# A four-layer transformer kernel: first tiles walked by halves, GpSimd's additions spread, squares moved, small squares by blocks, another table of steps

## What is computed

```python
def first_block(x, ...):                                  # layers 0 and 1
    for l in range(DEPTH):
        proj = x @ w_in[l]
        hq, hf, hi, hg, nq, kc, vc, ks, vs, kw, vw, gt = jnp.split(proj, pts, axis=-1)
        o_a = hgrn2_mixer(hq, hf, hi, hg, lbs[l], hg_norm_w[l])   # gated linear recurrence, 4 heads of 128
        o_b = nsa_mixer(nq, kc, vc, ks, vs, kw, vw, gt, ...)      # compressed, selected and window attention
        mix = jnp.concatenate([o_a, o_b], axis=-1) @ w_out[l]
        x = layer_norm(ALPHA * x + mix, ln1_g[l], ln1_b[l])
        ffn = (jax.nn.silu(x @ w_ffn_gate[l]) * (x @ w_ffn_up[l])) @ w_ffn_down[l]
        x = layer_norm(ALPHA * x + ffn, ln2_g[l], ln2_b[l])

def second_block(x, ...):                                 # layers 2 and 3
    for layer in range(DEPTH):
        h = rmsnorm(x, attn_norm[layer])
        ...                                               # q, k, v (and the index network in layer 2)
        x = x + mixed @ w_o[layer]
        h = rmsnorm(x, ffn_norm[layer])
        x = x + conv_ffn(h, w_up[layer], conv_w[layer], conv_b[layer], w_down[layer])   # width 2816
    return rmsnorm(x, final_norm)
```

## Time and profile before

| what | before |
|---|---|
| median of 3 runs | 1427.36 us (1426.35 to 1429.48) |
| profiled execution, its own time | 1427.59 us |
| its span | 1425.8 us |
| mean granted clock of TensorE | 0.989 |
| busy share: TensorE, VectorE, ScalarE, GpSimd | 96%, 67%, 51%, 6% |
| DMA | 233 MB, 164 GB/s |

### The profile page before, as it was taken

How to read it: one execution, slowest core, us unless ns; L and a number is a source line. 1 busy time by engine, 2 the same in 40 slices (tenths; PEclk the granted TensorE clock), 3 DMA queues, 4 the chain that set the end, 5 groups by cost and what they waited for, 6 DMA issues and landing times.

```text
span 1425.8 us, 24726 instructions
## 1 busy us (share of the span) xinstructions
PE 1368.6 (96%) x10094; PEld 1257.3 (88%) x10094; DVE 956.0 (67%) x1624; ACT 729.5 (51%) x1216; POOL 84.1 (6%) x79
## 2 busy tenths in 40 slices
PE   9998899999999988999998999999999999999998
PEld 7997689999899868999988988889999998889997
DVE  5676775555759576655565786687777655687776
ACT  4755444333475644343354555655546555655554
POOL 0330000000004100000000011220000000000000
PEclk9999999999999999999998999999999999999999
DMA  8752245555443314655534434445554534545541
GB/s 315 280 179 78 87 155 194 185 178 181 155 196 120 118 60 148 212 195 183 178 122 159 149 119 148 140 174 178 182 192 167 202 105 145 191 154 201 180 177 59
DMA packets 38632, 233.24 MB, mean 164 GB/s; under 512 B 5016, under 2 KB 8808, under 8 KB 12152
## 3 DMA queue, kind: packets, MB, share of 16 engines
q1 hardware_dynamic: 36456, 224.18, 45.2%
q0 software_dynamic: 2064, 7.47, 1.6%
HBM read 230.55 MB, written 1.09 MB: 162 GB/s over the span
## 4 chain that ended last, share of the span: by engine, by line
PE 81%; DVE 11%; ACT 4%; issue 2%; DMA 1%; POOL 0%; SPq 0%; DVEq 0%; ACTq 0%
PE bank L776 20%; PE bank L777 19%; PE bank L778 19%; PE bank L784 4%; PE bank L785 4%; PE bank L788 4%; DVE w_lo L603 3%; PE bank L899 2%; PE bank L984 1%; ACT w_hi L593 1%; PE bank L1006 1%; PE bank L1019 1%; DVE arena L1755 1%; DVE heads_buf L1588 1%; DVE x L1704 1%
## 5 line engine op out<-in xcount | busy, mean ns | idle before, releaser
L603 DVE TENSOR_TENSOR w_lo<-raw,w_hi 128x1024 fp32r<-128x1024 f32 x404 | 483.7, 1236 | 99.7 <-ACT w_hi L593 95.3
L776 PE MATMUL bank<-a_hi,w_hi 128*128 128x256 f32 x1856 | 529.8, 285 | 6.6 <-DVE w_lo L603 6.1
L777 PE MATMUL bank<-a_lo,w_hi 128*128 128x256 f32 x1856 | 525.8, 283 | 0.0
L778 PE MATMUL bank<-a_hi,w_lo 128*128 128x256 f32 x1856 | 525.6, 283 | 0.0
L593 ACT ACTIVATE w_hi<-raw 128x1024 fp32r<-128x1024 f32 x404 | 406.3, 1050 | 94.5 <-PE bank L778 67.4
L776 PEld LDWEIGHTS bank<-a_hi,w_hi 128*128 128x128 f32 x1856 | 356.6, 192 | 12.3 <-issue 8.9
L777 PEld LDWEIGHTS bank<-a_lo,w_hi 128*128 128x128 f32 x1856 | 356.8, 192 | 1.3
L778 PEld LDWEIGHTS bank<-a_hi,w_lo 128*128 128x128 f32 x1856 | 356.7, 192 | 0.0
L1755 DVE SCALAR_TENSOR_TENSOR arena<-bank,conv_col,arena 128x254 f32<-128x254 f32 (+1 forms) x176 | 76.7, 477 | 51.8 <-ACT arena L1313 50.1
L784 PE MATMUL bank<-w_hi,a_hi 128*128 128x256 f32 (+1 forms) x320 | 100.6, 335 | 5.9 <-ACT a_hi L619 2.3
L777 PE MATMUL bank<-w_lo,h_hi 128*128 128x512 f32 x264 | 105.2, 399 | 0.0
(11 more groups left out here) (266 smaller groups left out, 1892.1 us busy)
## 6 DMA issues: line engine op xcount, KB each, us to landing
raw<-in_stream SPq DMA_DIRECT2D x201, 1024.0 KB, 4.9
bias_t<-bias_rows SPq DMA_DIRECT2D x6, 512.0 KB, 6.9
heads_buf<-in_w SPq DMA_DIRECT2D x2, 1024.0 KB, 8.0
gains<-in_w SPq DMA_DIRECT2D x2, 1024.0 KB, 10.0
gains<-in_ln_g POOLq DMA_DIRECT2D x4, 512.0 KB, 4.2
gains<-in_ln_b POOLq DMA_DIRECT2D x4, 512.0 KB, 5.9
gains<-in_rms_g POOLq DMA_DIRECT2D x3, 512.0 KB, 4.3
res<-in_xT SPq DMA_DIRECT2D x4, 256.0 KB, 5.0
```

Source lines behind the costliest of these rows:

```text
L603: dve.tensor_tensor(w_lo[:, i % PARTS, half_tile(h)], raw[:, i % SLOTS, half_tile(h)], w_hi[:, i % PARTS, half_tile(h)].bitcast(F32), ALU. ...
L776: pe.matmul(out, lh, rh, start=first, stop=False)
L777: pe.matmul(out, lh, rl, start=False, stop=False)
L778: return pe.matmul(out, ll, rh, start=False, stop=last)
```

## The change

The table of steps changes in all four layers; the order of the weight stream does not. `WARM` goes from 7 to 4. `first_rows` becomes `first_tiles`: tile hi0 for both row halves together, by halves of the weight tile, all products with the high weight part before those with the low one; tile hi1 in the same way for the first and then the second row half. The last warm-up matmul leaves its sum open, and tile hi0 adds to the zeros. At levels 2 and 3 (halves of 64 and 32) only the kept blocks are multiplied: 8 matmuls of 64 x 64 and 16 of 32 x 32 instead of 8 of 128 x 128. At the norm between layers 1 and 2 ScalarE squares after one weight tile's split instead of after two. GpSimd's addition h waits for hidden tile 3 + h of layer 2's feed-forward part.

```diff
--- before.py
+++ after.py
@@ -37,7 +37,7 @@
 SLOTS = 3
 X_PARTS = 4
 HID_PARTS = 4
-WARM = 7
+WARM = 4
 PARTS = 3
 HSLOTS = 6
 HEAD = 2
@@ -91,33 +91,33 @@
     0: """
         a hf0, b hf0, a hf1, b hf1, a hq0, gates, b hq0, logs, a hq1, sums, b hq1, a kskw, decay 1, b kskw,
         a nq0, decay 2, level 0, b nq0, level 1, a kcvc, level 2, b kcvc, level 3, a hg0, level 4, b hg0,
-        level 5, gt, a hg1, level 6, b hg1, hid 0, level 7, hid 1, level 8, silu, a vsvw, hid 2, phase
-        heads, hid 3, ho 0, ho 1, b vsvw, hidT, a nq1, gtT, S 0, kcv, S 1, ho_out, b nq1, oT 0, T 0, phase
+        gt, level 5, a hg1, level 6, b hg1, hid 0, level 7, hid 1, level 8, silu, a vsvw, hid 2, phase
+        heads, ho 0, hid 3, b vsvw, ho 1, hidT, a nq1, S 0, kcv, S 1, gtT, ho_out, b nq1, oT 0, T 0, phase
         out, oT 1, out 0 0 0, S 2, T 1, out 0 0 1, V 0, V 1, S 3, out 1 0 0, T 2, S 4, phase out1, out 1 0
-        1, cs, V 2, T 3, out 0 1 0, V 3, S 5, out 0 1 1, T 4, cT, S 6, out 1 1 0, V 4, co 0, co 1, out 1 1
-        1, T 5, S 7, mT 2, V 5, T 6, out 2 0 0, out 2 0 1, T 7, out 2 1 0, V 6, V 7, mT 3, out 2 1 1""",
+        1, cs, V 2, T 3, out 0 1 0, V 3, S 5, out 0 1 1, cT, T 4, S 6, out 1 1 0, V 4, co 0, co 1, T 5, S 7,
+        mT 2, out 1 1 1, V 5, T 6, out 2 0 0, out 2 0 1, T 7, out 2 1 0, V 6, V 7, out 2 1 1, mT 3""",
     1: """
-        a hf0, b hf0, a hf1, b hf1, a hq0, gates, logs, b hq0, a hq1, b hq1, sums, a kskw, b kskw, a nq0, b
-        nq0, decay 1, level 0, decay 2, a kcvc, level 1, b kcvc, level 2, a hg0, level 3, b hg0, gt, level
-        4, a hg1, level 5, level 6, hid 0, b hg1, level 7, a vsvw, silu, level 8, hid 1, hid 2, phase heads,
-        ho 0, b vsvw, ho 1, hid 3, gtT, S 0, hidT, S 1, a nq1, ho_out, kcv, b nq1, T 0, phase out, oT 0, S
-        2, out 0 0 0, oT 1, V 0, T 1, out 0 0 1, out 1 0 0, V 1, S 3, T 2, S 4, out 1 0 1, phase out1, cs, V
-        2, out 0 1 0, S 5, T 3, out 0 1 1, T 4, V 3, S 6, cT, V 4, out 1 1 0, out 1 1 1, co 0, T 5, mT 2, co
-        1, V 5, S 7, T 6, out 2 0 0, T 7, V 6, out 2 0 1, V 7, out 2 1 0, mT 3, out 2 1 1""",
+        a hf0, b hf0, a hf1, b hf1, a hq0, gates, logs, b hq0, a hq1, b hq1, a kskw, sums, b kskw, a nq0,
+        decay 1, b nq0, level 0, decay 2, a kcvc, level 1, b kcvc, level 2, a hg0, level 3, b hg0, gt, hid
+        0, level 4, a hg1, level 5, level 6, b hg1, level 7, a vsvw, silu, level 8, hid 1, hid 2, phase
+        heads, ho 0, gtT, b vsvw, ho 1, hid 3, S 0, hidT, S 1, a nq1, ho_out, kcv, b nq1, T 0, phase out, oT
+        0, S 2, out 0 0 0, oT 1, V 0, T 1, out 0 0 1, out 1 0 0, V 1, S 3, T 2, S 4, out 1 0 1, phase out1,
+        cs, V 2, out 0 1 0, S 5, T 3, out 0 1 1, T 4, V 3, S 6, cT, V 4, out 1 1 0, out 1 1 1, co 0, T 5, mT
+        2, co 1, V 5, S 7, T 6, out 2 0 0, T 7, V 6, out 2 0 1, V 7, out 2 1 0, mT 3, out 2 1 1""",
     2: """
         phase tiles, kw, a qi0, b qi0, kwT, a qi1, b qi1, a qi2, kiT, b qi2, I 0, I 1, a qi3, b qi3, I 2, I
-        3, a q0, b q0, I 4, I 5, a k0, I 6, b k0, I 7, S 0, a q1, choose 0 2, b q1, T 0, choose 0 2, a k1, S
-        1, V 0, choose 0 2, b k1, T 1, S 2, a q2, choose 0 2, V 1, choose 1 2, T 2, b q2, V 2, choose 1 2, S
-        3, a k2, b k2, choose 1 2, choose 1 2, unsel, a v2, T 3, S 4, V 3, b v2, T 4, a q3, S 5, V 4, b q3,
-        T 5, a k3, V 5, mT 0, b k3, a v3, S 6, mT 1, b v3, out 0 0 0, phase out, S 7, out 0 0 1, T 6, out 1
-        0 0, out 1 0 1, V 6, mT 2, T 7, phase out1, out 0 1 0, out 0 1 1, V 7, out 1 1 0, out 1 1 1, mT 3,
+        3, a q0, I 4, b q0, I 5, a k0, I 6, I 7, b k0, S 0, a q1, choose 0 2, b q1, choose 0 2, T 0, a k1, S
+        1, choose 0 2, choose 0 2, b k1, V 0, S 2, T 1, a q2, V 1, T 2, b q2, choose 1 2, V 2, choose 1 2, S
+        3, a k2, b k2, choose 1 2, T 3, a v2, choose 1 2, unsel, V 3, S 4, b v2, T 4, a q3, S 5, V 4, b q3,
+        T 5, a k3, V 5, mT 0, b k3, a v3, S 6, b v3, mT 1, phase out, S 7, out 0 0 0, T 6, out 0 0 1, out 1
+        0 0, out 1 0 1, mT 2, V 6, T 7, phase out1, out 0 1 0, out 0 1 1, V 7, out 1 1 0, out 1 1 1, mT 3,
         out 2 0 0, out 2 0 1""",
     3: """
-        phase tiles, a q0, b q0, a k0, b k0, S 0, a q1, b q1, T 0, a k1, S 1, b k1, V 0, T 1, S 2, V 1, a
-        q2, b q2, S 3, T 2, a k2, b k2, T 3, S 4, a v2, V 2, V 3, b v2, T 4, a q3, V 4, S 5, b q3, T 5, a
-        k3, mT 0, b k3, V 5, S 6, a v3, b v3, mT 1, phase out, S 7, T 6, out 0 0 0, out 0 0 1, out 1 0 0,
-        out 1 0 1, V 6, mT 2, out 0 1 0, T 7, phase out1, out 0 1 1, V 7, out 1 1 0, out 1 1 1, mT 3, out 2
-        0 0, out 2 0 1""",
+        phase tiles, a q0, b q0, a k0, b k0, a q1, S 0, b q1, T 0, a k1, S 1, V 0, b k1, T 1, S 2, V 1, a
+        q2, b q2, S 3, T 2, a k2, b k2, T 3, S 4, a v2, V 2, V 3, b v2, T 4, a q3, V 4, S 5, b q3, a k3, T
+        5, mT 0, b k3, V 5, S 6, a v3, b v3, mT 1, phase out, S 7, T 6, out 0 0 0, out 0 0 1, out 1 0 0, out
+        1 0 1, out 0 1 0, V 6, mT 2, T 7, phase out1, out 0 1 1, V 7, out 1 1 0, out 1 1 1, mT 3, out 2 0 0,
+        out 2 0 1""",
 }
 
 
@@ -815,21 +815,31 @@
                     mm = high_first(out, tiles[4 * q:4 * q + 4], lambda: wait_drained(pe, turned), q == 0, q == 1)
                 return mm
 
-            def first_rows():
-
-
-                b = open_bank((0, "hi0"))
+            def first_tiles():
+
+
+
+                banks = [open_bank((0, name)) for name in HEAD_TILES[0]]
                 pe.wait_ge(zeroed, 1)
-                for _ in range(WARM):
-                    pe.matmul(b[:, 0:512], s_hg[:, 0:P], s_hg[:, 0:512], start=True, stop=True)
-                w = [part[:, 0, :].rearrange("p (k c) -> p k c", k=KT) for part in (w_hi, w_lo)]
-                for k in range(KT):
-                    if k % 2 == 0:
-                        pe.wait_ge(a_lo_done, k // 2 + 1)
-                    if k % 4 == 0:
-                        pe.wait_ge(w_lo_done, k // 4 + 1)
-                    products(b[:, 0:S], (a_hi[:, k, 0:P], a_lo[:, k, 0:P]), [part[:, k, :] for part in w],
-                             k == 0, k == KT - 1)
+                for n in range(WARM):
+                    pe.matmul(banks[0][:, 0:512], s_hg[:, 0:P], s_hg[:, 0:512], start=True, stop=n < WARM - 1)
+                for i, rows in ((0, (0, 1)), (1, (0,)), (1, (1,))):
+                    high, low = [part[:, i, :].rearrange("p (k c) -> p k c", k=KT) for part in (w_hi, w_lo)]
+                    for h in range(2):
+                        pe.wait_ge(w_hi_done, 2 * i + h + 1)
+                        places = [(k, slice(tt * P, (tt + 1) * P), banks[i][:, tt * S:(tt + 1) * S])
+                                  for k in range(4 * h, 4 * h + 4) for tt in rows]
+                        for n, (k, t, out) in enumerate(places):
+                            if i == 0 and n % 4 == 0:
+                                pe.wait_ge(a_lo_done, k // 2 + 1)
+                            pe.matmul(out, a_hi[:, k, t], high[:, k, :], start=i > 0 and k == 0, stop=False)
+                            pe.matmul(out, a_lo[:, k, t], high[:, k, :], start=False, stop=False)
+                        pe.wait_ge(w_lo_done, 2 * i + h + 1)
+                        for k, t, out in places:
+                            mm = pe.matmul(out, a_hi[:, k, t], low[:, k, :], start=False,
+                                           stop=(k, t.start) == (KT - 1, rows[-1] * P))
+                    if rows[-1] == NT - 1:
+                        close_bank(mm)
 
             def behind_norm_tiles(n, keys, heads):
 
@@ -896,7 +906,13 @@
                         continue
                     for st in range(NT):
                         c = h * S + st * P
-                        mm = pe.matmul(out[:, c:c + P], lhs[:, c:c + P], rhs[:, c:c + P], start=True, stop=True)
+                        if half not in BY_BLOCKS:
+                            mm = pe.matmul(out[:, c:c + P], lhs[:, c:c + P], rhs[:, c:c + P], start=True, stop=True)
+                            continue
+                        for at in range(0, P, 2 * half):
+                            keys, queries = slice(c + at, c + at + half), slice(c + at + half, c + at + 2 * half)
+                            mm = pe.matmul(out[at:at + half, queries], lhs[:, keys], rhs[:, queries],
+                                           start=True, stop=True)
                 mm.then_inc(product_done, 1)
 
             def compress(l, part):
@@ -1141,11 +1157,7 @@
                 if l > 0:
                     pe.wait_ge(acc_drained, 2 * l * PIECES)
 
-            first_rows()
-            half_of_tile((0, "hi0"), True)
-            for name in HEAD_TILES[0][1:]:
-                half_of_tile((0, name), False)
-                half_of_tile((0, name), True)
+            first_tiles()
 
             pe.wait_ge(start_in, STARTS)
             b = open_bank(("cmpbias",))
@@ -1275,10 +1287,13 @@
                 keys, turn = norm_tail(l, kind), norms[-1]
                 act.activation(nstat[:, 0, 18:19], eps_ln[:, 0:1], ACT.Sqrt)
```

(8 more changed lines are left out.)

## The result

| what | before | after |
|---|---|---|
| median | 1426.86 us (4 runs, 1423.35 to 1429.48) | 1414.59 us (4 runs, 1413.50 to 1416.32) |
| profiled execution; its span | 1427.59; 1425.8 us | 1413.50; 1411.7 us |
| mean granted clock | 0.989 | 0.991 |

The ratio is 0.9915, with a 95% interval of 0.9897 to 0.9933: faster by 12.3 us, where 11.1 were predicted. The two profiled executions lie 14.1 us apart: that of the changed kernel is its fastest run, and that of the kernel before lies 0.7 us above its median.

A forecast was written before the change was run, and what follows sets the result against it. TensorE, with a matmul in flight 96% of the span, was taken as the bound. Terms -2.8 - 1.9 - 2.2 - 1.1 - 3.1 = -11.1 from 1427.59 gave 1416.4 us for the median; range 1412.5 to 1420, widened to 1410.5 to 1421.5.

The forecast's parts named there:

- start: First tiles: fewer warm-ups and a new product order bring line 1156 from 22.36 to about 19.5 us; -2.8 us.
- squares: Levels with halves of 64 and 32: multiplying only kept blocks saves 1.9 us over two layers, mostly at 64.
- norm: Between layers 1 and 2: squaring after one split starts the transposes 2.1 us earlier, head tiles 2.3; term -2.2 us.
- additions: Layer 2's feed-forward part: spreading GpSimd's additions stops them slowing VectorE ahead of h_hi; -1.1 us.
- table: Attention parts of all four layers: reordered steps cover TensorE's waits, -1.0, -0.5, -1.2, -0.4 by layer; -3.1 us.
- the idle pieces of 0.7 and 0.3 us: First tile: TensorE idles 0.7 us for the next a_lo part and 0.3 us for the second high half.
- at 0.055 ... the 32-level 1.76 (saves 0.03): Squares: at 0.055 us a record, from two nearest rows, the 32-level costs 1.76 us and saves only 0.03.
- The low end, -3.6: Squares, two layers: if cost went with columns (0.028 us a record), the 32-level would save 0.89 too; -3.6 us.
- The bound of -4: Norm between layers 1 and 2: less idle time may also avoid the first of two clock drops, each up to 1.7 us.
- the other fourteen or so are hidden by VectorE's idle quarter: Layer 2's feed-forward part: from up6 on splits are 3 us and more ahead, so the remaining spread additions cost nothing.
- the wait at T 4: Layer 2 attention: the softmax of S 4, which had 1.5 us of cover before T 4, has none.
- T 0 now has 2.9 us where it needs about 3.5: Layer 3 attention: T 0 has too little time behind S 0, set against 0.7 us gained at S 0; net -0.4.

The follow-up runs named there:

- experiment 7: Changed kernel with experiment 6's edit, plus only 32 x 32 diagonal blocks multiplied in ten of the twelve masked levels: 1408.60 us, ratio 0.9870.
- Experiment 5: Changed kernel with both high weight splits ahead of the squares again at the norm between layers 1 and 2: 1417.85 us, ratio 0.9935.
- experiment 4: Changed kernel with GpSimd's sixteen additions in one block again: 1416.00 us, ratio 0.9920.
- experiment 8: Kernel before the change with only the new table of steps: 1423.62 us beside 1429.19, ratio 0.9970.
- experiment 6: Changed kernel with layer 0's mT 3 back ahead of the last output piece (out 2 1 1): 1414.30 us, ratio 0.9914.
- experiment 3: Changed kernel with the former table of steps in all layers: 1420.65 us, ratio 0.9957.
- experiment 1: Changed kernel with the start undone (seven warm-up matmuls, first tile row half after row half): 1418.06 us, ratio 0.9938.
- experiment 2: Changed kernel with whole 128 x 128 squares at levels 2 and 3 again: 1418.77 us, ratio 0.9938.
- experiment 9: Changed kernel with 45 unused identity matmuls filling TensorE's idle time ahead of transposes at four norms: 1412.37 us, ratio 0.9890.

## Why the prediction was nearly right, and where not

The forecast of 1416.4 lies 1.8 us above the median and inside its range; the mechanism (each part takes a wait or columns away, and nearly all of it arrives) held. One term was clearly mis-sized: the squares saved 3.4 us by the rows, not 1.9, which is nearly the whole miss. The other rows stand within 0.3 us of their terms, two of them by errors that cancel.

| term | predicted | undone, by medians (by ratios) | gain in the pair of traces |
|---|---|---|---|
| start | -2.8 | 3.5 (3.3) | 2.8 at the small product |
| squares | -1.9 | 4.2 (3.3) | 1.7 a layer |
| norm | -2.2 | 3.3 (2.9) | 2.2 at the first set, 2.5 at the second |
| additions | -1.1 | 1.4 (0.7) | 0.8 over the part (undone 0.15) |
| table | -3.1 | 6.1 (6.0), alone 4.3 | -0.1, 0.9, 1.4, 0.9 in layers 0 to 3 |

The last column adds up to about 12.5 us. The other 1.6 of the 14.1 come where both kernels run the same code and their clock drops lie differently: 0.7 from the middle of layer 1 on (6.9 to 7.6), 0.9 behind the second set (10.2 to 11.0).

**Start: right in the sum, partly by luck.** 19.59 against 19.5, and the small loads had landed. But the first tile starts at 7.67, not at 6.88: the weight loads of the last warm-ups are still 0.86 us apart (5.32, 6.17, 7.03), while those of the kernel before were 0.43 apart from 6.03 on, so the clock rose later in this run. And the idle pieces of 0.7 and 0.3 us that I counted did not come: from 8.19 to 19.59 the 95 products stand 0.12 us apart. The two errors cancel.

**Squares: the step "at 0.055 ... the 32-level 1.76 (saves 0.03)" failed.** I carried the spacing of two nearest rows, 0.055 us, to a shape unlike both: the level of 32 takes 0.70 us. The 64 level was near (1.15 against 0.88 + 0.22 of tail). The low end, -3.6, went with columns at 0.028 a record, which was too dear for the 32 level too; the 3.4 us that arrived lie just inside it. What differs is where the results go. The blocks of the 64 level all write the same partitions of PSUM (0 to 63), those of the 32 level two groups of 32 in turn, those of experiment 7 all four, and the spacing falls from 0.062 to 0.016 to 0.009 us. The two 32 x 32 cases differ only in the number of groups, and each group keeps one pace: 2 x 0.016 = 0.032 us, 4 x 0.009 = 0.036. The starts of the single records in the traces agree: within a pair or a four they are 0.007 us apart, and a new pair comes every 0.032 us in the changed kernel, a new four every 0.032 us in the first half of experiment 7's 64. So blocks in different groups overlap; the same shape in one group alone was not run.
The Trainium skill speaks on both sides. TensorE: Matmul & The Clock Gate, "Back-to-back issue gap", has some 62 ns (25 at best) as the spacing that small matmuls don't go below: the 64 level agrees, 0.016 and 0.009 us don't, and the measurement decides. TensorEngine Tiling (Array Packing), "Key Properties", says that tiles at different places of the array work in parallel, and the two small spacings agree. I weighed only the first of the two.

**Norm: right in mechanism and size.** The idle 2.01 us are gone as worked out, and the two sets come 2.2 and 2.5 us earlier; the head tiles wait 0.71 us behind their transposes, not none. "The second set still waits over 4 us": 5.13. The bound of -4 named the clock, but took both drops for 3.4 us; the second was 6.8 (0.79 over 24 us is 10 us at half clock). Experiment 5 has a drop over the head products that the changed kernel has not, which is one reason for its 3.3.

**Additions: the waits right, the sum too high.** 0.67 us where "near 0.7" stood, and the new wait at up5's low part is 0.23 us where up to 0.75 was allowed for. But the step "the other fourteen or so are hidden by VectorE's idle quarter" failed in part: of the 0.84 us that experiment 4's wait shows, 0.15 arrive at the end of the part, and 0.8 of the kernel before's 1.5.

**Table: the sum near, the parts less so.** In layer 0 the predicted -1.0 does not show in the pair of traces, where the changed kernel's clock is at half over the last output tile; by itself the table gains 0.75 at the end of that layer (experiment 8, 369.43 against 370.18). mT 3 costs 1.1 us at its wait where 0.9 stood, and 0.7 net (experiment 6). In layer 1 it is -0.9 (6.9 - 4.3 - 1.7) where -0.5 stood. In layer 2 -1.2 was near, at 1.4, though not for the reasons given: the wait at T 4 that I counted against it did not come, while S 0, which I did not count, waits 0.73. In layer 3 "T 0 now has 2.9 us where it needs about 3.5" was wrong: no wait there, -0.9.

**What stays open.** The five undone parts add up to 18.5 us by medians, 16.2 by ratios, and the whole change is worth 12.3. The changed kernel's own time stands in all five differences, so an error of 1 us in it makes 4 in that excess, and its ratio is known to 2.6 us: the excess isn't clear of noise. For the table a part of it may be real: 4.3 alone (2.4 to 6.1), 6.1 on top of the rest, with two new waits of 1.9 us together in experiment 3. For the others the clock mixes in. A drop lasts 3.4 or 6.8 us inside these traces, and its place differs even ahead of the changed part: experiment 4 runs the same code as the changed kernel up to layer 2's feed-forward part, and is already 1.5 us off there. The same steps from the second set between layers 1 and 2 to the middle of layer 2 take 146.9 us in the changed kernel, with 3.4 us of half clock at their start, 147.4 to 148.4 in experiments 1, 2, 4 and 6 with 6.8 us, and 146.0 in experiment 9 with none. How much of this is the edit and how much chance needs more profiles of one kernel.

## What to carry to other kernels

Undo each part by itself, and follow the same instruction in both traces to the end of the stage, not only to the wait: the additions took 0.8 us off a wait and 0.15 off their part (experiment 4), mT 3's place 1.1 us off a wait and 0.7 off its layer (experiment 6). Before two waits are compared, look whether the clock was the same in both windows; in experiment 6 it was not, and the waits alone mislead. Price a shape that the trace doesn't show by running it once, where it can be multiplied in the kernel; here the guess of 0.055 us for a record hid 1.5 us in the term and another 5.7 us in the levels next to the changed ones. Differences of 1 to 2 us on 1414 want medians over many runs or the rows of the stage itself, never the end of two single traces.

## What was unexpected of the hardware

- Plain float32 matmuls of 32 x 32 blocks on the diagonal: 64 records in 0.76 us (0.009 us apart), 32 records on two of the four partition groups in 0.70 (0.016), while 16 of 64 x 64, all to the same partitions, take 1.15 (0.062).
- An addition of 128 x 256 on GpSimd is 0.97 us long in a block and 1.58 to 1.66 us when it starts beside VectorE's splits, and four splits are 5.17 instead of 4.62 us: both sides pay.
- 45 matmuls of no use, put into idle time, raised the mean granted clock from 0.991 to 0.996. Each 0.001 would be worth at most 1.4 us; 7 us of clock gave back only about 2.2 us. That the drops lie mostly where TensorE waits anyway is the likely reason.
